# Modulation slabs regrouped between the norms and the up projection, and VectorE's work reordered in the last recurrent turn

## The reference

```python
# first_block
h = rmsnorm(x, g[0])
y = hybrid_mixer(h, ...)      # in projection; attention heads, gating, recurrent (RWKV) heads
x = x + rmsnorm(y, g[1])
h = rmsnorm(x, g[2])
y = memory_cross_attention(h, rmsnorm(mem, ...), ...)
x = x + rmsnorm(y, g[3])
h = rmsnorm(x, g[4])
y = conv_ffn(h, w_up, conv_w, conv_b, w_down)   # up: 2048 -> 2 x 5632
# second_block, each of the layers l = 0, 1
sh, sc, g = split(silu(c) @ w_mod[l] + b_mod[l], 3)      # w_mod[l]: 2048 x 6144
hl = xl * (1 + sc) + sh
```

## Time and profile before

| | us |
|---|---|
| median of 3 runs (lowest, highest) | 3083.79 (3081.26, 3092.01) |
| the profiled execution | 3083.16 |
| its span in the profile | 3081.4 |
| TensorE busy | 2999.9 |
| VectorE busy | 1669.2 |
| ScalarE busy | 1352.9 |
| mean granted TensorE clock | 0.992 |

### The profile page before, as it was taken

One profiled execution on the slowest core, in us unless ns is written; L12 is line 12 of the kernel. 1 busy time (PEld: TensorE's weight loads), 2 busy tenths in 40 slices (PEclk: granted clock), 3 DMA queues, 4 the chain that ended last, 5 costly groups with the idle time before them and its releaser, 6 DMA issues.

```text
span 3081.4 us, 48573 instructions
## 1 busy us (share of the span) xinstructions
PE 2999.9 (97%) x19912; PEld 2539.2 (82%) x19912; DVE 1669.2 (54%) x2561; ACT 1352.9 (44%) x2084; POOL 43.8 (1%) x84
## 2 busy tenths in 40 slices
PE   8999988999899999999999999999999999999997
PEld 7888876898588778788888887788888998889996
DVE  5666565544766666564464324554562574247754
ACT  5333334434455445454453224444442471245643
POOL 1000000000000000000000000000000000000000
PEclk9999998999999999999999999999999999999998
DMA  7665655356565777745553222222233452234442
GB/s 254 229 219 210 217 194 209 123 175 249 216 219 192 271 263 248 271 164 186 179 190 104 96 95 70 82 82 93 82 129 108 164 166 94 96 120 151 145 160 106
DMA packets 73800, 510.18 MB, mean 166 GB/s; under 512 B 8325, under 2 KB 8465, under 8 KB 19601
## 3 DMA queue, kind: packets, MB, share of 16 engines
q1 hardware_dynamic: 63504, 435.74, 41.3%
q0 software_dynamic: 10112, 71.73, 6.0%
HBM read 503.23 MB, written 6.55 MB: 165 GB/s over the span
## 4 chain that ended last, share of the span: by engine, by line
PE 92%; DVE 5%; ACT 1%; DMA 1%; issue 0%; SPq 0%; ACTq 0%; DVEq 0%
PE bank L767 21%; PE bank L711 16%; PE bank L710 7%; PE bank L1467 6%; PE bank L1469 6%; PE bank L1468 6%; PE bank L910 3%; PE bank L942 3%; PE bank L911 2%; PE bank L912 2%; PE bank L1050 2%; PE bank L808 2%; PE bank L809 1%; PE bank L810 1%; PE bank L1117 1%; PE bank L1505 1%
## 5 line engine op out<-in xcount | busy, mean ns | idle before, releaser
L2285 DVE TENSOR_TENSOR ring_f32r<-ring_f,high_f32r 128x1024 fp32r<-128x1024 f32 (+1 forms) x738 | 830.5, 1163 | 762.7 <-ACT high_f32r L1642 738.1
L1642 ACT CAST high_f32r<-ring_f 128x1024 fp32r<-128x1024 f32 (+1 forms) x644 | 609.3, 994 | 848.7 <-PE bank L767 461.1
L711 PE MATMUL bank<-hyz_f32r,high_f32r 128*128 128x512 f32 x2112 | 751.4, 400 | 3.8 <-DVE hyz_f32r L2285 3.8
L710 PE MATMUL bank<-hyz_f32r,ring_f32r 128*128 128x256 f32 x2008 | 564.2, 281 | 1.6 <-DVE ring_f32r L2285 0.9
L767 PE MATMUL bank<-hyz_f32r,high_f32r 128*128 128x512 f32 (+1 forms) x2016 | 533.7, 342 | 5.2 <-DVE hyz_f32r L2285 3.0
L711 PEld LDWEIGHTS bank<-hyz_f32r,high_f32r 128*128 128x128 f32 x2112 | 393.8, 188 | 122.1 <-issue 34.9
L767 PE MATMUL bank<-hyz_f32r,ring_f32r 128*128 128x512 f32 (+1 forms) x1184 | 410.4, 347 | 0.0
L767 PEld LDWEIGHTS bank<-hyz_f32r,high_f32r 128*128 128x128 f32 x2016 | 347.4, 190 | 49.3 <-issue 6.2
L710 PEld LDWEIGHTS bank<-hyz_f32r,ring_f32r 128*128 128x128 f32 x2008 | 379.8, 189 | 7.4 <-DVE ring_f32r L2285 1.6
L1467 PE MATMUL bank<-hyz_f32r,high_f32r 128*128 128x512 f32 (+1 forms) x1024 | 359.3, 351 | 3.1 <-DVE ring_f32r L2285 3.1
L1469 PE MATMUL bank<-hyz_f32r,ring_f32r 128*128 128x512 f32 (+1 forms) x1024 | 344.7, 337 | 0.0
(11 more groups left out here) (415 smaller groups left out, 4024.0 us busy)
## 6 DMA issues: line engine op xcount, KB each, us to landing
ring_f<-in_w_in SPq DMA_DIRECT2D x159, 1024.0 KB, 4.9
ring_f<-in_w_up SPq DMA_DIRECT2D x88, 1024.0 KB, 4.9
ring_f<-in_w_out SPq DMA_DIRECT2D x56, 1024.0 KB, 4.9
ring_f<-in_w_mod SPq DMA_DIRECT2D x48, 1024.0 KB, 4.9
ring_f<-in_w_down SPq DMA_DIRECT2D x64, 704.0 KB, 4.1
h_f<-in_w_mod POOLq DMA_DIRECT2D x38, 1024.0 KB, 6.9
ring_f<-in_w_kv SPq DMA_DIRECT2D x8, 1024.0 KB, 5.3
z_f<-in_w_mod POOLq DMA_DIRECT2D x8, 1024.0 KB, 7.8
```

Of the source, the lines that this page charges most:

```text
L710: mm(small, lo, x_hi, start=False, stop=False)
L711: last = mm(bank, hi, pair(x_hi, x_lo), start=start, stop=stop)
L1642: act.copy(w_hi[p % 2][:, half], slot[s % SLOTS][:, half]).then_inc(w_high, 1)
L2285: return v.tensor_tensor(out, in0, in1, op)
```

## The change

Slabs: 16 instead of 12 run in the norms (7, then three singly, then 6), from ten buffers instead of eight. The two new buffers lie in the second half of `x_all`. So the load of `ctxT`, which stood there, moves behind the first pair of slabs in up. Of the ten buffers six are used twice. The last two slabs lie where the third and fourth quarter of up's operand go, so ScalarE waits for all 16 slabs ahead of those two casts. The other 32 run in 16 pairs after up tiles 4, 11, ..., 53 and 62, 65, ..., 83, and POOL loads both buffers of a pair together. The copy of the first group's row moves from up tile 28 to the end of the operand's casts.

VectorE, last turn: the lowering of "42 second" moves ahead of the wait for the second gating sum, "43 first" stays, "43 second" goes ahead of the wait for the exponentials, "44 first" takes its place after `rw_hat`, and none is left after the first copy of `multiplied(1)`. First attention: `gather` and `variance` of `mem` go from after head pair 0 to after head pair 1, straight ahead of `inverted`.

```diff
-NORM_MODS = (8, 4)
-UP_MODS = [3, 6, 9, 12] + [32 + 3 * k // 2 for k in range(16)] + [62 + 4 * k // 3 for k in range(16)]
+NORM_MODS = 16
+UP_MODS = [4 + 7 * k for k in range(8)] + [62 + 3 * k for k in range(8)]
...
-        norm_mod = [arena[:, a + n * SLOT:a + (n + 1) * SLOT] for a, c in ((Z_AT + 16 * T, 4), (Y1_AT, 2), (H1_AT, 2)) for n in range(c)]
+        norm_mod = [arena[:, a + n * SLOT:a + (n + 1) * SLOT] for a, c in ((Z_AT + 16 * T, 4), (Y1_AT, 2), (H1_AT, 2), (X1_AT, 2)) for n in range(c)]
...
             pool.wait_ge(S("rows_loaded"), 32)
-            load(x_all[:, KC * T:], d["ctxT"], "rows_loaded")
+            for n in (8, 9):
+                load(norm_mod[n], d["w_mod"][48 + n, :, :], "rows_loaded")
             pool.wait_ge(S("c_out"), MEM_HEADS)
...
+            for n in range(8):
+                load(norm_mod[n], d["w_mod"][48 + n, :, :], "up_mod_loaded")
+            for n in range(10, 14):
+                pool.wait_ge(S("mod_read"), 48 + n - 9)
+                pool.wait_ge(S("up_mod_loaded"), 16 * 8)
+                load(norm_mod[n - 10], d["w_mod"][48 + n, :, :], "up_mod_loaded")
+            pool.wait_ge(S("rows_loaded"), 64)
+            for n in (14, 15):
+                pool.wait_ge(S("mod_read"), 48 + n - 9)
+                load(norm_mod[n - 10], d["w_mod"][48 + n, :, :], "rows_loaded")
             pool.wait_ge(rhs_split, RHS0["up"] + 4)
...
+            for n in range(NORM_MODS, 48, 2):
+                pool.wait_ge(S("mod_read"), 48 + n)
+                pool.wait_ge(S("up_mod_loaded"), 16 * (n - 4))
+                for m in range(2):
+                    load(up_mod[m], d["w_mod"][48 + n + m, :, :], "up_mod_loaded")
+                if n == NORM_MODS:
+                    load(x_all[:, KC * T:], d["ctxT"], "rows_loaded")
...
-            norm_mods(5)
+            norm_mods(7)
             colsum4(H[0], T, 7, lambda: norm_mods(1))
-            norm_mods(4)
+            norm_mods(6)
...
+                    n = NORM_MODS + 2 * UP_MODS.index(j)
+                    pe.wait_ge(S("up_mod_loaded"), 16 * (n - 2))
+                    for m in range(2):
+                        up_mod_matvec(48 + n + m, up_mod[m])
...
-            rhs_highs("up")
+            rhs_highs("up", range(2))
+            act.wait_ge(S("mod_read"), 48 + NORM_MODS)
+            rhs_highs("up", range(2, 4))
+            mod_row_copied(3, 4, up_mod_row)
...
                 if sgu:
+                    in1_lowered()
                     wait_sum()
...
-                in1_lowered(2)
+                in1_lowered(1 if sgu else 2)
...
                 step(tt(kn, kn, rinv))
+                if sgu:
+                    in1_lowered()
                 dve.wait_ge(S("rw_exp"), i + 1)
...
-                in1_lowered()
+                if not sgu:
+                    in1_lowered()
                 multiplied(2)
...
-                if i == 0:
+                if i == 1:
                     gather(T, 1)
                     variance(D, 1)
-                elif i == 1:
                     inverted()
```

More of the change, by code:

```diff
@@ L606, in _ @@
             pool.wait_ge(S("rows_loaded"), 32)
-            load(x_all[:, KC * T:], d["ctxT"], "rows_loaded")
+            for n in (8, 9):
+                load(norm_mod[n], d["w_mod"][48 + n, :, :], "rows_loaded")
             pool.wait_ge(S("c_out"), MEM_HEADS)
[L609 to L612, removed]
-            pool.wait_ge(rhs_split, RHS0["up"] + 4)
[L614 to L618, removed]
+            for n in range(8):
[8 more added lines that the diff above has]
+                load(norm_mod[n - 10], d["w_mod"][48 + n, :, :], "rows_loaded")
+            pool.wait_ge(rhs_split, RHS0["up"] + 4)
+            pool.wait_ge(S("rows_loaded"), 96)
+            for n in range(NORM_MODS, 48, 2):
[5 more added lines that the diff above has]
+                    load(x_all[:, KC * T:], d["ctxT"], "rows_loaded")
             def pool_stage(layer):
@@ L1392, in up_mod_matvec @@
                 mod_matvec(n, 4, slab)
-            norms = iter(range(sum(NORM_MODS)))
+            norms = iter(range(NORM_MODS))
             def norm_mods(count):
                 for n in itertools.islice(norms, count):
-                    pe.wait_ge(S("up_mod_loaded"), 16 * (NORM_MODS[0] if n < NORM_MODS[0] else sum(NORM_MODS)))
-                    up_mod_matvec(48 + n, norm_mod[n % NORM_MODS[0]])
+                    if n < 8:
+                        pe.wait_ge(S("up_mod_loaded"), 16 * 8)
+                    elif n < 10:
+                        pe.wait_ge(S("rows_loaded"), 64)
+                    elif n < 14:
+                        pe.wait_ge(S("up_mod_loaded"), 16 * 12)
+                    else:
+                        pe.wait_ge(S("rows_loaded"), 96)
+                    up_mod_matvec(48 + n, norm_mod[n % 10])
             tiles_summed("wo", 3, H[0])
             finish_sum(T, 7)
-            norm_mods(5)
+            norm_mods(7)
             colsum4(H[0], T, 7, lambda: norm_mods(1))
-            norm_mods(4)
+            norm_mods(6)
             for j in range(TILES["up"]):
@@ L1410, in _ @@
                 if j in UP_MODS:
-                    n = sum(NORM_MODS) + UP_MODS.index(j)
-                    pe.wait_ge(S("up_mod_loaded"), 16 * (n + 1))
-                    up_mod_matvec(48 + n, up_mod[n % 2])
+                    n = NORM_MODS + 2 * UP_MODS.index(j)
+                    pe.wait_ge(S("up_mod_loaded"), 16 * (n - 2))
+                    for m in range(2):
+                        up_mod_matvec(48 + n + m, up_mod[m])
                 if j in UP_TURNED:
@@ L2018, in _ @@
                 for j in range(4):
-                    if j == 0:
+                    if j == 0 and part:
                         mod_row_copied(3 + part, 4, up_mod_row)
@@ L2747, in _ @@
                 step(ts(part, part, 1.0, op0=ALU.add))
-            dve.wait_ge(S("rows_loaded"), 48)
+            dve.wait_ge(S("rows_loaded"), 112)
             dve.wait_ge(S("down_used"), 3 * 15 + 2)
```

## The result

The change is faster. Five runs of it have a median of 3067.15 us (3063.12 to 3068.98), beside 3083.79 before (five runs too), so the medians lie 16.6 us apart. The forecast was 3065.4, with a range of 3060 to 3074. The profiled execution took 3063.12 us, against 3083.16 before.

A forecast was written before the change was run, and what follows sets the result against it. Bound: TensorE's own work and some 80 us in which it stands. Terms 8.0 + 0.6 + 0 + 9.8 = 18.4 us off the profiled 3083.16 gave 3064.8; the median, 0.63 higher, 3065.4, range 3060 to 3074.

The forecast's parts named there:

- Last turn, 8.0 us: VectorE's new order of lowered halves lets the last turn's transposes begin 8.0 us earlier; bounds 2.3 and 8.5.
- the rival in which something else holds them: Last turn: a slab's load or VectorE's gating norm holds the transposes, only 2.5 us gained, 3070.9; chance 0.13.
- The new wait ahead of the products: Last turn: TensorE waits about 2 us for the operands of the turn's products, in place of two waits.
- the split into 2.2 for the first two waits, 3.8 for the third and 2 for the clock: Last turn: parts of the 8.0 us, from TensorE's waits for lowered halves and seven steps at full clock.
- a chain of short waits that moves as a whole: Behind the last turn's transposes: waits between TensorE, VectorE and ScalarE shift together, keeping the 8.0 us.
- First attention, 0.6 us: First attention heads: the wait of 2.35 us goes, the next product stays, the clock saves 0.6 us; bounds -1 and 3.4.
- the half of a difference between two cold restarts: First attention: one-piece restart saves half the difference between 5.4 and 6.7 us at the lower clock, 0.6 us.
- the rival in which the clock stays up: First attention: TensorE's clock does not fall, 2.8 us more gained, 3062.6; chance 0.10.
- Norms, 0: Norms: four more slabs fit inside TensorE's waits of 2.59 and 3.81 us, so up starts unchanged: 0 us.
- Up, 9.8 us: Up: 36 slabs at 1.18 us become 16 pairs at 1.18 + 0.86; 4.7 by four slabs gone, 5.1 by pairing.
- The rival with a dear second slab: Up: the second slab of a pair costs as much as the first, 5.1 us less gained, 3070.5; chance 0.10.
- Ring loads: Up: weight loads beside slabs cost nothing up to 13.7 us; rival: they starve, 3102 at 16 us, chance 0.03.

The follow-up runs named there:

- the slabs alone: The changed kernel with VectorE's old orders in last turn and first attention, so only the slabs are regrouped: 3073.68 us, 0.9966 to before.
- Third late: The changed kernel with the lowered half ahead of the exponentials put back behind the first copy: 3073.22 us, 0.9967 to before.
- First late: The changed kernel with "42 second" lowered behind the second gating sum again, beside "43 first": 3068.04 us, 0.9953 to before.
- both profiles of after: The changed kernel profiled in the main series (3067.15 us) and once more, unchanged, in a second series (3066.97 us, 0.9938 to before).
- the single slabs: The changed kernel with its last 32 slabs run one at a time in up instead of in 16 pairs: 3072.14 us, 0.9963 to before.
- the four in a row: The changed kernel with up's first 16 slabs as four groups of four, after tiles 6, 20, 34 and 48: 3068.94 us, 0.9948 to before.
- the last turn alone: The kernel before with only the four edits of VectorE's order in the last turn: 3079.00 us, 0.9976 to before.
- the attention alone: The kernel before with only `mem`'s gather and variance moved behind the second head pair: 3084.22 us, 0.9998 to before.
- the root later: The changed kernel with ScalarE taking the root of `mem`'s norm behind the second heads' copies: 3068.21 us, 0.9943 to before.

## Why the prediction was right

The time was forecast 1.75 us too low at the median, and the sum of 18.4 us stands against 17.8 in the profiles from the scan on. The two large terms came about as described, but that the sum is as close as 0.6 us is luck: 1.8 us more than forecast in up stand against 0.6 less in the attention and 1.7 lost behind up, and single profiles of equal code differ by up to 1.9 us at the second product. Point by point:

- **Last turn, 8.0 us.** Right at the transposes: 8.28 (7.6 against the slabs alone, which had the old order, a clock of 0.77 from 464 to 470 and its transposes at 28.40). So the rival in which something else holds them is out. The new wait ahead of the products was there, 1.36 instead of about 2 us, and the clock stayed at 1.00. What failed is the split into 2.2 for the first two waits, 3.8 for the third and 2 for the clock, as if each could be had by itself. Third late shows that they are one chain: VectorE's order puts "44 first" ahead of the masks only if "43 second" has already been lowered ahead of the exponentials. First late shows 1.85 us for the first half, given the third. And "a chain of short waits that moves as a whole" held to 0.4 us in both profiles of after (7.84 and 8.58 at the second product), but the single slabs and the four in a row, the same up to there, kept only 6.9 and 6.7, and 3.2 us were given back in the profile of the last turn alone. In all three the clock was below 1.00 between 495 and 515.
- **First attention, 0.6 us.** 0.0. The reason for the product's place, ScalarE's copy, was right, and the root's move shows it. What failed is the half of a difference between two cold restarts (the stretches at the lower clock behind a wait). In both profiles of after, the restart behind this product was as cold as before: 0.54 from 521 to 528 in the first and 0.55 from 525 to 532 in the second, against 0.52 from 531 to 538. In the attention alone it was 0.71, and that gained nothing at up. So the rival in which the clock stays up is out too. The step was sized from two windows of one profile, and the clock falls differently from one to the next.
- **Norms, 0.** Right: the distance from second product to up's start is 268.45 us before and 268.44 after. The slabs came in time: TensorE waits for none in the norms, and ScalarE's last two casts wait for VectorE (1.73 and 1.62 us), not for a slab.
- **Up, 9.8 us.** 11.6, mis-sized by 1.8. The prices were right: 36 x 1.19 = 42.8 before, 16 x 2.05 = 32.8 after, 10.0 us. The rest is the tile behind a pair, 5.55 instead of 5.65 us, 16 times. The rival with a dear second slab, 8.0 us for a tile with a pair, is ruled out. The Trainium skill, page "TensorEngine Tiling (Array Packing)", section "Tiling Modes", says that a change of the tiling mode drains TensorE. These tiles agree with it, as a group costs 0.33 us beyond its slabs whether it has one slab, two or four; that the drain is what costs them was not tested.
- **Ring loads.** They did slow: beside a pair to 7.9 us at most, beside four slabs to 9.7, beside a pair and `ctxT` to 10.7 (10.9 in the second profile), beside four slabs and `ctxT` to 12.5. The 5.4 of before that the prediction starts from holds for 1000 to 1300 alone; over all of up it was 7.4 there. The prediction's estimate of 10.8 comes from queues that take turns (the Trainium skill, page "DMA: Bandwidth & Descriptors", section "SWDGE vs HWDGE vs iDMA"); a pair alone stayed below it. None reached 13.7, and TensorE did not wait.
- **Not foreseen, 1.7 us lost behind up.** TensorE waits 2.1 us for ScalarE at the end of down in both kernels. TensorE's timeline and windows there, of after and then of before:

```profile
1578.89 1.22 PE L1439 MATMUL bank<-z_f,rest_f 128*128 128x256 f32 x2 [2.11 <-ACT z_f L2077]
```

```profile
1570.00:1580.00 10.00, 7.89 (x42) 6.57 (x41) 7.74 (x23) 2.46 (x5) 0.00 (x0) 0.94 0.84 288
1580.00:1590.00 10.00, 10.00 (x43) 8.62 (x42) 9.15 (x16) 8.36 (x14) 1.08 (x2) 0.89 0.17 71
```

```profile
1600.61 0.70 PE L1421 MATMUL bank<-z_f,rest_f 128*128 128x256 f32 x2 [2.12 <-ACT z_f L2056]
```

```profile
1592.00:1602.00 10.00, 7.88 (x43) 6.63 (x42) 7.89 (x24) 2.51 (x5) 0.00 (x0) 1.00 0.85 291
1602.00:1612.00 10.00, 10.00 (x48) 8.80 (x47) 9.43 (x16) 8.83 (x14) 1.08 (x2) 1.00 0.22 89
```

The wait is the same, but in after the clock fell behind it: (1 - 0.94) x 10 + (1 - 0.89) x 10 = 1.7 us. The code there is unchanged. From the same matmul of down (1335.90 in after, 1357.67 in before) to the end, before took 1723.7 us, and both profiles of after, third late, the single slabs and the slabs alone took 1725.4 to 1725.5. But it is no mark of the change. The last turn alone, with the old slabs, lost the clock at this wait too and took 1725.0. The four in a row and the root later, which have the change, kept a clock of 1.00 there, lost it at two later places (0.83 over 10 us each) and took 1726.9 and 1727.0; the attention alone kept it as well and took 1722.7. So equal code takes 1722.7 to 1727.0 us here, by where the clock falls. What decides that was not tried, and whether the 1.7 us come with the change or by chance stays open.

## What to carry to other kernels

When an engine waits several times for pieces that another one makes in a fixed order, don't price the waits one by one: find the one place in the producer's list from which the others follow, and count the cold restart with it. Small products of another array shape, put between the tiles of a large one, were cheapest in groups (1.19 us for the first slab, 0.86 for each further one), as long as their loads arrive. And before filling an idle stretch with more transfers, look at the DMA share there: at 1.01 an earlier request changed nothing.

## What the hardware showed that was not expected

- The start of the program varies: the scan in the last turn began at 437.3 to 443.9 us, in kernels equal up to there. Two single profiles can differ by 6.6 us before the change begins.
- A wait of 2.1 us may or may not be followed by a lower clock, with the same code on both sides (0.94 and 0.89, or 1.00), for 1.7 us. It was in ten of the fourteen profiles.
- The tile of up behind a pair takes 5.55 us instead of 5.65, evenly over its 16 steps. The first tile behind each turned row (6.54 us) does so too, and the second one behind the rows at tiles 29 and 85. The tile behind four slabs does not, nor the one behind a single slab, but for one of the single slabs' kernel (tile 32, 5.54). This is the same in every profile that has such tiles, and its cause stays open.
